# Taking the two VectorE operations on a finished attention part apart: subtraction two chunks behind, addition four

## The chip, the cores and the metric

The kernel runs on one core of one Trainium2 chip. The metric is the device time of one execution in microseconds (us), the lower the better. The kernel before was timed in three runs: median 3198.25 us, from 3195.41 to 3200.84 us.

## What is computed

One inference step of a two-layer encoder over 1024 prompt positions and 32 sample positions (1056 columns), in fp32 throughout. Layer 0 has latent attention with 16 heads, layer 1 forgetting attention with 16 heads. For this change only the core of both matters:

```
sc = q @ k.T + bias, masked
pr = softmax(sc, axis=-1)
o  = pr @ v          # one block of 64 rows per head
y  = o @ w_o         # the projection behind attention
```

After it come a gated feed-forward block of inner width 2816 and a gated per-layer embedding, in both layers.

## The kernel before, in words

**Numbers as two halves.** To keep fp32 accuracy the kernel splits each factor of a matmul into a rounded high half and the remainder (`act_hi`, `act_lo`). A product is then three matmuls (`three`, L1034 to L1036: high by high, low by high, high by low).

**Tiles, steps, heads, pairs.** In attention a head is cut into nine query tiles, 0 to 7 of 128 prompt rows and tile 8 of the 32 sample rows. They are taken in the order 7, 6, 8, 0, 5, 4, 1, 2, 3 (`ORDER`, L178), one per *step*. Two heads of nine steps make a *pair* (18 steps); the pairs run in a hardware loop (`pair`, one copy on each engine: L1245 TensorE, L1696 ScalarE, L2256 VectorE). The first pair stands ahead of the loop, and a short *drain* finishes the last head behind it.

**One step's way.** TensorE makes the scores of a tile in PSUM banks 0 to 3 (`scores`, L1155). VectorE takes the negated row maximum (`neg_max`, L2227), ScalarE the exponential with its row sum (`exps`, L1678, tile `probs`), VectorE the reciprocal of the sum (L2235), GpSimd scales the row (L931). The scores of a later tile may only enter a bank when the exponential that last read it is done (`pe.wait_ge(at_e, ...)`, L1163): tile 1 goes into bank 2, which the exponential of tile 5 frees one and a half steps earlier.

**Chunks.** The scaled probabilities must be turned before they can be multiplied with v. That is done in 11 *chunks* per head of up to four 128x128 blocks: chunks 0 to 3 belong to tiles 6 and 7, chunk 4 to tile 8, chunks 5 to 7 to tiles 4 and 5, chunk 8 to tiles 0 and 1, chunks 9 and 10 to tiles 2 and 3. TensorE turns a chunk into bank 4 or 5 (`turn`, L1208), ScalarE rounds it to its high half (`hi`, L1687, tile `probs_t_hi`), VectorE makes the low half (`lo`, L2240, tile `probs_t_lo`), and TensorE multiplies both halves with v (`pv`, L1232) into bank 6 or 7, `PV_LAG` = 2 chunks behind the turn. `RUN_STEPS` says in which step a chunk is handled; a head's chunks run on into the next head's steps, so chunks 5 to 10 of one head are handled in steps 0 to 4 of the next. Below, a chunk number with a dash (0') is of that next head.

**Leaving attention.** After chunks 4, 7 and 10 a *part* of the head's output stands complete in PSUM (32 columns in bank 6, 512 in bank 7, 512 in bank 6), as 128 rows: 64 from the high half of v, 64 from the low half. `OUT_LAG` = 2 chunks behind, ScalarE copies the upper 64 rows, rounded, to `act_hi` (`outs`, L1690 to L1694). VectorE's own `outs` (L2243) then does two operations, both reading PSUM: `out_partial` = low rows minus `act_hi` (L2252), and `act_lo` = high rows plus `out_partial` (L2254). Between them stands a wait on `at_oadd`, which the subtraction raises, as the addition reads what it wrote. The addition raises `at_olo`. TensorE waits for `at_olo` before it begins to fill a bank again (L1221): chunk 0' of the next head needs part 7 gone from bank 7, chunk 8 needs part 4 gone from bank 6, chunk 4' needs part 10 gone from it. The projection behind attention waits for the last `at_olo` (L1423).

**VectorE's order.** Within a step: `neg_max` of the step's tile, the reciprocal of the step before, then for each of the step's chunks c: `lo(c)`, `outs(c - 2)`. So the two operations on part 4 stand behind `lo(6)`, those on part 7 behind `lo(9)`, and those on part 10 behind `lo(1')` and ahead of `lo(2')`. Behind part 7's two comes `neg_max` of tile 5. Each engine works off its list in that order.

Of the kernel before, what the change touches and what calls it, by code (L numbers as in the profile page):

```python
# [15 lines left out]
F32 = mybir.dt.float32  # L16
F32R = mybir.dt.float32r
ACT = mybir.ActivationFunctionType
ALU = mybir.AluOpType
# [5 lines left out]
SEQ, DEC, PAST = 1024, 32, 256  # L25
# [7 lines left out]
H = 16  # L33
Q_RANK, KV_RANK, NOPE, ROPE, VD = 512, 256, 64, 32, 64
# [144 lines left out]
STEPS = len(ORDER)  # L179
PAIR = 2 * STEPS  # L180
TURN_SLOTS = 4
PV_LAG, OUT_LAG = 2, 2
RUNS = [(6, 7), (8,), (4, 5), (0, 1), (2, 3)]
RUN_STEPS = [5, 6, 6, 7, 8, 9, 10, 11, 12, 12, 13]
DRAIN = 5
# [14 lines left out]
HC = len(CHUNKS)  # L200
# [100 lines left out]
def build_program(nc, io):  # L301
    with ExitStack() as ctx:
# [14 lines left out]
        nh, o = at("act_hi", [P, KD, T], F32R, o)  # L317
# [161 lines left out]
        at_oadd = sem("at_o_lo_added")  # L479
# [70 lines left out]
        def last_tile(c):  # L550
            return max(chunk(c)[0], key=ORDER.index)

        def out_part(c, i, buf, half=0):

            tile = last_tile(c)
            hp = c // HC
            rows = slice(64 * (hp % 2), 64 * (hp % 2) + 64)
            pair = i + (-1 if c < 0 else 0)
            part = OUT_AFTER[tile]
            of = slice(half * VD, (half + 1) * VD)  # L560
            cols, src = ((slice(SEQ, T), ps[of, 6, 0:DEC]) if tile == 8 else
                         (slice(512, SEQ), ps[of, 7, :]) if tile > 3 else (slice(0, 512), ps[of, 6, :]))
            return buf[rows, pair, cols], src, 3 * hp + part + 1

        def score_tile(tile):
            M = P if tile < 8 else DEC
# [2 lines left out]
        def is_out(c):  # L569
            return chunk(c)[3] and last_tile(c) in OUT_AFTER  # L570
# [1455 lines left out]
        def _(dve):  # L2026
# [193 lines left out]
            def attention(layer):  # L2220
                base_n, base_c = layer * H * STEPS, layer * H * HC

                def neg_max(i, s):
                    k, tile = s % STEPS, ORDER[s % STEPS]
                    M = P if tile < 8 else DEC
                    dve.wait_ge(at_s, i * PAIR + (base_n + s + 1))
                    V.tensor_reduce(nmx[0:M, k:k + 1], score_tile(tile), AX.X, ALU.max, negate=True).then_inc(at_nm, 1)  # L2227

                def invert(i, s, first):
                    k, tile = s % STEPS, ORDER[s % STEPS]  # L2230
                    M = P if tile < 8 else DEC
                    dve.wait_ge(at_e, i * PAIR + (base_n + s + 1))
                    if not (first and s < STEPS):
                        dve.wait_ge(at_p, i * PAIR + (base_n + s - STEPS + 1))
                    V.reciprocal(rinv[0:M, k:k + 1], rsum[0:M, k:k + 1]).then_inc(at_r, 1)  # L2235

                def lo(i, c):
                    dve.wait_ge(at_hi, i * (2 * HC) + (base_c + c + 1))
                    for (dst, src), (hi, _) in zip(turned(c, ptl), turned(c, pth)):
                        last = V.tensor_tensor(dst, src, hi.bitcast(F32), ALU.subtract)  # L2240
                    last.then_inc(at_lo, 1)

                def outs(i, c):  # L2243
                    if is_out(c):
                        dst, src, n = out_part(c, i, nl)
                        dve.wait_ge(at_ohi, i * 6 + (3 * layer * H + n))
                        hp, src_cols = c // HC, src.shape[-1]
                        part = osum[64 * (hp % 2):64 * (hp % 2) + VD, 0:src_cols]
                        _, src_lo, _ = out_part(c, i, nl, 1)
                        if not (isinstance(i, int) and i == 0 and n == 1):  # L2250
                            dve.wait_ge(at_olo, i * 6 + (3 * layer * H + n - 1))
                        V.tensor_tensor(part, src_lo, out_part(c, i, nh)[0].bitcast(F32), ALU.subtract).then_inc(at_oadd, 1)  # L2252
                        dve.wait_ge(at_oadd, i * 6 + (3 * layer * H + n))
                        V.tensor_tensor(dst, src, part, ALU.add).then_inc(at_olo, 1)  # L2254

                def pair(i, first, drain=False):  # L2256
                    for s in range(DRAIN if drain else PAIR):
                        if not drain:
                            neg_max(i, s)
                        todo = [s - 1] if (s >= 1 or not first) and not (drain and s > 0) else []  # L2260
                        while todo:
                            invert(i, todo.pop(), first)
                        for c in chunks_at(s):
                            if c >= 0 or not first:
                                lo(i, c)
                            if c >= OUT_LAG or not first:
                                outs(i, c - OUT_LAG)
                    if drain:
                        for c in range(-OUT_LAG, 0):
                            outs(i, c)  # L2270

                pair(0, True)
                with dve.Fori(1, H // 2) as i:
                    pair(i, False)
                pair(H // 2, False, True)
# [530 lines left out]
```

## Time and profile before

| | us |
|---|---|
| median of three runs (lowest, highest) | 3198.25 (3195.41, 3200.84) |
| the profiled execution | 3194.3 |
| its span | 3192.5 |
| TensorE matmul busy | 3006.4 (94%) |
| VectorE busy | 2026.4 (63%) |
| GpSimd busy | 1428.1 (45%) |
| ScalarE busy | 982.6 (31%) |
| mean granted TensorE clock | 0.974 of full |

The shares are means over stages with different limits. Attention takes two stretches of the span, about 282 to 590 us (layer 0) and 1824 to 2128 us (layer 1); the feed-forward blocks take most of the rest, with TensorE busy throughout. In the rows below the time of an instruction and its length stand first; in square brackets is how long its engine sat idle before it, and what ended that.

### The profile page before, as it was taken

Reading aid. Unit: us, or ns where it says so; the run is one execution under the profiler, and the core shown is the slowest. Engines: PE = TensorE matmul, PEld = TensorE weight load, DVE = VectorE, ACT = ScalarE, POOL = GpSimd, SP = SyncE. Lnnn points to the kernel's source line nnn. Section 1 sums busy time; section 2 is a strip of 40 time slices with the busy share of each in tenths; the row PEclk is TensorE's granted clock in tenths of the full one; section 3 lists DMA queues with packets and bytes.
Section 4 is the critical chain, followed back from the end, with each engine's and each line's share of the span. In section 5 each row is a group of like instructions: output and inputs, shape, how many; then the busy total and the mean of one; then the engine's idle time right before and its main releaser. Section 6 shows DMA issues by size and latency. Waiting matters only on the chain.

```text
span 3192.5 us, 54358 instructions
## 1 busy us (share of the span) xinstructions
PE 3006.4 (94%) x18978; PEld 2905.2 (91%) x18978; DVE 2026.4 (63%) x3685; ACT 982.6 (31%) x2197; POOL 1428.1 (45%) x933
## 2 busy tenths in 40 slices
PE   8999999999999999998989999889899999999887
PEld 7889888888999999998878888889899999999887
DVE  4566888465655565567565588855655655565675
ACT  4234777342000000004442277753300000000252
POOL 4233545464333343345554455545533333343563
PEclk9999999999999999999999999999899999999998
DMA  3497444211111111111103666522011111111111
GB/s 111 178 316 242 123 122 126 98 40 47 40 53 39 46 53 39 46 46 61 40 21 127 187 138 140 130 81 73 28 53 44 42 53 39 46 52 40 48 54 55
DMA packets 163132, 264.63 MB, mean 83 GB/s; under 512 B 95057, under 2 KB 108897, under 8 KB 162641
## 3 DMA queue, kind: packets, MB, share of 16 engines
q1 hardware_dynamic: 163024, 263.21, 26.8%
q8 instruction: 66, 1.08, 0.1%
q14 instruction: 42, 0.34, 0.0%
HBM read 197.74 MB, written 65.42 MB: 82 GB/s over the span
## 4 chain that ended last, share of the span: by engine, by line
PE 78%; DVE 9%; issue 4%; ACT 4%; POOL 3%; DMA 1%; SPq 0%; DVEq 0%; ACTq 0%; POOLq 0%
PE ps L1324 30%; PE ps L1034 12%; PE ps L1035 12%; PE ps L1036 12%; PE ps L1232 4%; PE ps L1208 3%; POOL pre_sums L891 1%; DVE sublayer_out L2058 1%; PE ps L1180 1%; DVE neg_max L2227 1%; DVE out_partial L2252 1%; PE ps L1055 1%; PE ps L1181 1%; PE ps L1069 1%; ACT probs_t_hi L1687 1%
## 5 line engine op out<-in xcount | busy, mean ns | idle before, releaser
L855 POOL TENSOR_TENSOR weight_hi<-weight_raw,ones 128x1024 fp32r<-128x1024 f32 x179 | 354.9, 1982 | 1169.0 <-PE ps L1036 598.8
L2295 DVE TENSOR_TENSOR sublayer_out<-ps,sublayer_out 128x352 f32<-128x352 f32 x1008 | 527.8, 524 | 516.4 <-PE ps L1036 507.9
L1324 PE MATMUL ps<-act_hi,weight_hi 128*128 128x352 f32 x2112 | 686.1, 325 | 10.1 <-ACT ffn_act L1735 4.8
L1324 PE MATMUL ps<-act_hi,weight_lo 128*128 128x352 f32 x2112 | 683.8, 324 | 0.0
L1324 PE MATMUL ps<-act_lo,weight_hi 128*128 128x352 f32 x2112 | 683.7, 324 | 0.0
L869 POOL TENSOR_TENSOR weight_lo<-weight_raw,weight_hi 128x1024 fp32r<-128x1024 f32 x193 | 477.1, 2472 | 54.9 <-ACT weight_hi L1725 28.1
L1034 PE MATMUL ps<-act_hi,weight_hi 128*128 128x352 f32 (+2 forms) x1392 | 469.7, 337 | 29.6 <-DVE weight_lo L2102 11.4
L1035 PE MATMUL ps<-act_lo,weight_hi 128*128 128x352 f32 (+2 forms) x1392 | 457.1, 328 | 0.0
L1036 PE MATMUL ps<-act_hi,weight_lo 128*128 128x352 f32 (+2 forms) x1392 | 456.8, 328 | 0.0
L931 POOL TENSOR_TENSOR probs<-probs,row_inv 128x1024 f32<-128x1024 f32 (+8 forms) x288 | 311.0, 1092 | 322.8 <-DVE row_inv L2235 321.6
L1324 PEld LDWEIGHTS ps<-act_hi,weight_hi 128*128 128x128 f32 x2112 | 399.2, 189 | 14.4 <-issue 6.9
L1324 PEld LDWEIGHTS ps<-act_lo,weight_hi 128*128 128x128 f32 x2112 | 400.0, 189 | 0.4 <-issue 0.2
L1324 PEld LDWEIGHTS ps<-act_hi,weight_lo 128*128 128x128 f32 x2112 | 399.9, 189 | 0.5 <-issue 0.2
L1034 PEld LDWEIGHTS ps<-act_hi,weight_hi 128*128 128x128 f32 (+2 forms) x1392 | 266.4, 191 | 37.4 <-issue 22.7
L1035 PEld LDWEIGHTS ps<-act_lo,weight_hi 128*128 128x128 f32 (+2 forms) x1392 | 266.9, 192 | 4.9 <-issue 1.1
L1036 PEld LDWEIGHTS ps<-act_hi,weight_lo 128*128 128x128 f32 (+2 forms) x1392 | 266.0, 191 | 2.4
L1735 ACT ACTIVATE ffn_act<-ps 128x352 f32<-128x352 f32 x132 | 61.3, 465 | 619.3 <-DVE ps L2299 619.2
L2240 DVE TENSOR_TENSOR probs_t_lo<-ps,probs_t_hi 128x512 fp32r<-128x512 f32 (+3 forms) x384 | 210.8, 556 | 47.3 <-ACT probs_t_hi L1687 41.2
L1678 ACT ACTIVATE probs<-ps,neg_max 128x1024 f32<-128x1024 f32 (+8 forms) x288 | 204.9, 711 | 105.9 <-DVE neg_max L2227 104.6
L2227 DVE TENSOR_REDUCE neg_max<-ps 128x1 f32<-128x1024 f32 (+8 forms) x288 | 205.9, 715 | 34.5 <-PE ps L1185 32.7
L1232 PE MATMUL ps<-probs_t_hi,v_both 128*128 128x256 f32 (+3 forms) x736 | 212.6, 309 | 12.5 <-DVE probs_t_lo L2240 11.4
L1687 ACT ACTIVATE probs_t_hi<-ps 128x512 fp32r<-128x512 f32 (+3 forms) x384 | 184.5, 490 | 66.8 <-PE ps L1208 48.1
(177 smaller groups left out, 5763.1 us busy)
## 6 DMA issues: line engine op xcount, KB each, us to landing
weight_raw<-units SPq DMA_DIRECT2D x201, 512.0 KB, 3.3
k_hi<-kB_hi SPq DMA_DIRECT2D x32, 328.0 KB
qA_hi<-stage_hi SPq DMA_DIRECT2D x16, 528.0 KB, 3.4
qA_lo<-stage_lo SPq DMA_DIRECT2D x16, 528.0 KB, 4.5
q_hi<-qA_hi SPq DMA_DIRECT2D x16, 528.0 KB
q_lo<-qA_lo SPq DMA_DIRECT2D x16, 528.0 KB
kA_hi<-stage_hi SPq DMA_DIRECT2D x8, 656.0 KB, 3.0
kA_lo<-stage_lo SPq DMA_DIRECT2D x8, 656.0 KB, 4.7
```

The source lines that it names most:

```text
L855: pool.tensor_tensor(wh[:, slot, :], wraw[:, slot, :], ones[:, 0:1].to_broadcast((P, UW)), ALU.mult).then_inc(w_hi[slot], 1)
L869: pool.tensor_tensor(wl[:, slot, :], wraw[:, slot, :], wh[:, slot, :].bitcast(F32), ALU.subtract).then_inc(w_rdy[slot], 1)
L931: pool.tensor_tensor(p, p, rinv[0:M, k:k + 1].to_broadcast((M, KEYS[tile])), ALU.mult).then_inc(at_p, 1)
L1034: nc.tensor.matmul(out, ah, bh, start=first, stop=False)
L1035: nc.tensor.matmul(out, ah, bl, start=False, stop=False)
L1036: return nc.tensor.matmul(out, al, bh, start=False, stop=last)
L1232: mm = nc.tensor.matmul(out, halves, p.rearrange("p t q -> p (t q)") if n > 1 else p[:, 0, :], start=kt == 0 and h == 0, stop=ends and j + ...
L1324: mm = nc.tensor.matmul(ps[:, 3 * slot + b, 0:TB], a, x, start=(k == 0 and pas == 0), stop=(k == KD - 1 and pas == 2))
L1687: last = nc.scalar.activation(dst, src, ACT.Copy)
L2227: V.tensor_reduce(nmx[0:M, k:k + 1], score_tile(tile), AX.X, ALU.max, negate=True).then_inc(at_nm, 1)
L2240: last = V.tensor_tensor(dst, src, hi.bitcast(F32), ALU.subtract)
L2295: V.tensor_tensor(y[:, m, c], src, y[:, m, c], ALU.add).then_inc(f_acc, 1)
```

## The change

The subtraction stays where it was, two chunks behind. The addition gets a lag of its own, four chunks, and is issued behind `lo(c)` and ahead of the subtraction of the same turn. Semaphores and their counts stay; ScalarE's and TensorE's programs are not touched. The addition on part 4 now stands behind `lo(8)`, that on part 7 behind `lo(0')`, that on part 10 behind `lo(3')`. The drain issues the addition on part 7 behind its last `lo`.

```diff
-PV_LAG, OUT_LAG = 2, 2
+PV_LAG, OUT_LAG, LOW_LAG = 2, 2, 4
...
+        def out_sum(c):
+
+            rows = slice(64 * (c // HC % 2), 64 * (c // HC % 2) + VD)
+            return osum[rows, 0:DEC if last_tile(c) == 8 else 512]
...
-                def outs(i, c):
+                def out_partial(i, c):
+
+                    if is_out(c):
+                        _, src_lo, n = out_part(c, i, nl, 1)
+                        dve.wait_ge(at_ohi, i * 6 + (3 * layer * H + n))
+                        if not (isinstance(i, int) and i == 0 and n == 1):
+                            dve.wait_ge(at_olo, i * 6 + (3 * layer * H + n - 1))
+                        V.tensor_tensor(out_sum(c), src_lo, out_part(c, i, nh)[0].bitcast(F32),
+                                        ALU.subtract).then_inc(at_oadd, 1)
+
+                def out_low(i, c):
+
                     if is_out(c):
                         dst, src, n = out_part(c, i, nl)
-                        dve.wait_ge(at_ohi, i * 6 + (3 * layer * H + n))
-                        hp, src_cols = c // HC, src.shape[-1]
-                        part = osum[64 * (hp % 2):64 * (hp % 2) + VD, 0:src_cols]
-                        _, src_lo, _ = out_part(c, i, nl, 1)
-                        if not (isinstance(i, int) and i == 0 and n == 1):
-                            dve.wait_ge(at_olo, i * 6 + (3 * layer * H + n - 1))
-                        V.tensor_tensor(part, src_lo, out_part(c, i, nh)[0].bitcast(F32), ALU.subtract).then_inc(at_oadd, 1)
                         dve.wait_ge(at_oadd, i * 6 + (3 * layer * H + n))
-                        V.tensor_tensor(dst, src, part, ALU.add).then_inc(at_olo, 1)
+                        V.tensor_tensor(dst, src, out_sum(c), ALU.add).then_inc(at_olo, 1)
...
                         for c in chunks_at(s):
                             if c >= 0 or not first:
                                 lo(i, c)
+                            if c >= LOW_LAG or not first:
+                                out_low(i, c - LOW_LAG)
                             if c >= OUT_LAG or not first:
-                                outs(i, c - OUT_LAG)
+                                out_partial(i, c - OUT_LAG)
                     if drain:
-                        for c in range(-OUT_LAG, 0):
-                            outs(i, c)
+                        for c in range(-LOW_LAG, 0):
+                            out_low(i, c)
+                            if c + LOW_LAG - OUT_LAG < 0:
+                                out_partial(i, c + LOW_LAG - OUT_LAG)
```

## Rows read from the trace of the kernel before

**Rows 1.** The page: busy time of each engine, its share of the span, instructions

```profile
PE 3006.4 (94%) x18978; PEld 2905.2 (91%) x18978; DVE 2026.4 (63%) x3685; ACT 982.6 (31%) x2197; POOL 1428.1 (45%) x933
```

**Rows 2.** Waits in attention of layer 0: total us, times, longest us

```profile
PE ps L1034 <- ACT probs L1678: 11.8, 16, 1.2
```

**Rows 3.** Waits in attention of layer 1, same columns

```profile
PE ps L1180 <- ACT probs L1678: 22.5, 16, 2.1
```

**Rows 4.** Timeline of VectorE, layer 0, a pair's first head: start, length

```profile
359.94 0.69 DVE L2240 TENSOR_TENSOR probs_t_lo<-ps,probs_t_hi 128x512 fp32r<-128x512 f32 x1 [0.94 <-ACT probs_t_hi L1687]
360.67 0.69 DVE L2252 TENSOR_TENSOR out_partial<-ps,act_hi 64x512 f32<-64x512 f32 x1
361.49 0.68 DVE L2254 TENSOR_TENSOR act_lo<-ps,out_partial 64x512 f32 x1
362.20 0.96 DVE L2227 TENSOR_REDUCE neg_max<-ps 128x1 f32<-128x768 f32 x1
...
364.71 0.69 DVE L2240 TENSOR_TENSOR probs_t_lo<-ps,probs_t_hi 128x512 fp32r<-128x512 f32 x1
365.31 0.41 DVE L2227 TENSOR_REDUCE neg_max<-ps 128x1 f32<-128x256 f32 x1
```

**Rows 5.** The same in the pair's second head

```profile
379.53 0.69 DVE L2252 TENSOR_TENSOR out_partial<-ps,act_hi 64x512 f32<-64x512 f32 x1
...
380.96 0.94 DVE L2227 TENSOR_REDUCE neg_max<-ps 128x1 f32<-128x768 f32 x1
```

**Rows 6.** Timeline of TensorE in the first head, and one stall of the second

```profile
364.24 0.39 PE L1034 MATMUL ps<-k_hi,q_hi 128*128 128x256 f32 x1 [1.03 <-ACT probs L1678]
...
366.00 0.36 PE L1232 MATMUL ps<-probs_t_hi,v_both 128*128 128x256 f32 x1
...
369.14 0.35 PE L1232 MATMUL ps<-probs_t_hi,v_both 128*128 128x256 f32 x1 [0.27 <-DVE probs_t_lo L2240]
...
382.97 0.39 PE L1034 MATMUL ps<-k_hi,q_hi 128*128 128x256 f32 x1 [0.43 <-ACT probs L1678]
```

**Rows 7.** Timeline of VectorE, layer 1, a pair's second head

```profile
1926.41 0.69 DVE L2240 TENSOR_TENSOR probs_t_lo<-ps,probs_t_hi 128x512 fp32r<-128x512 f32 x1 [0.22 <-ACT probs_t_hi L1687]
...
1929.82 0.67 DVE L2240 TENSOR_TENSOR probs_t_lo<-ps,probs_t_hi 128x512 fp32r<-128x512 f32 x1
...
1932.86 1.22 DVE L2227 TENSOR_REDUCE neg_max<-ps 128x1 f32<-128x1024 f32 x1 [0.49 <-PE ps L1185]
```

**Rows 8.** Timeline of TensorE in that head

```profile
1925.95 0.38 PE L1180 MATMUL ps<-k_hi,q_hi 128*128 128x256 f32 x1 [1.10 <-ACT probs L1678]
...
1927.60 0.36 PE L1232 MATMUL ps<-probs_t_hi,v_both 128*128 128x256 f32 x1
...
1930.64 0.35 PE L1232 MATMUL ps<-probs_t_hi,v_both 128*128 128x256 f32 x1 [0.59 <-DVE probs_t_lo L2240]
```

**Rows 9.** Timeline of TensorE, layer 1: stalls of first and of second heads, in turn

```profile
1907.21 0.58 PE L1180 MATMUL ps<-k_hi,q_hi 128*128 128x256 f32 x1 [1.82 <-ACT probs L1678]
...
2055.78 0.38 PE L1180 MATMUL ps<-k_hi,q_hi 128*128 128x256 f32 x1 [1.81 <-ACT probs L1678]
...
2074.25 0.38 PE L1180 MATMUL ps<-k_hi,q_hi 128*128 128x256 f32 x1 [1.10 <-ACT probs L1678]
...
2092.82 0.39 PE L1180 MATMUL ps<-k_hi,q_hi 128*128 128x256 f32 x1 [1.81 <-ACT probs L1678]
...
2110.67 0.38 PE L1180 MATMUL ps<-k_hi,q_hi 128*128 128x256 f32 x1 [1.10 <-ACT probs L1678]
```

**Rows 10.** Windows behind these stalls: busy by engine, then granted clock, DMA share, GB/s

```profile
1907.21:1911.21 4.00, 4.00 (x21) 4.00 (x22) 2.78 (x7) 3.15 (x8) 2.68 (x2) 0.57 0.05 11
...
1925.95:1929.95 4.00, 4.00 (x32) 3.80 (x32) 3.45 (x9) 3.58 (x9) 2.68 (x2) 1.00 0.35 81
...
2092.82:2096.82 4.00, 4.00 (x32) 3.81 (x32) 3.53 (x8) 3.73 (x9) 2.68 (x2) 1.00 0.34 77
```

**Rows 11.** Timeline of VectorE in layer 0's drain

```profile
587.12 0.56 DVE L2240 TENSOR_TENSOR probs_t_lo<-ps,probs_t_hi 128x384 fp32r<-128x384 f32 x1
```

## The prediction

> **What bounds the kernel now.** I read the page first: TensorE is busy for 94% of the span, VectorE for 63% [rows 1]. That is a mean. In the feed-forward stages TensorE has no gap to give, and the change issues nothing there. So I went on to the waits of the two attention stretches, the only place where L2252 and L2254 run. There TensorE waits in every head for the exponential that frees its score bank: 11.8 us in 16 times in layer 0 [rows 2], 22.5 us in 16 times in layer 1 [rows 3]. ScalarE in turn was released by `neg_max`. What holds `neg_max` back? The timeline of VectorE shows it: `lo(9)` at 359.94, the subtraction on part 7 at 360.67, its addition at 361.49, and only then `neg_max` of tile 5 at 362.20 [rows 4], whose scores had long been there. TensorE takes up the scores of tile 1 at 364.24, after 1.03 us of idling, and stalls again, 0.27 us, at 369.14, where `pv` waits for `lo(2')` [rows 6], which stands behind part 10's two operations in the same way. I call these site A (behind part 7) and site B (behind part 10). The pattern repeats through both layers: at A a pair's first head (7 of them per layer, as the first pair has nothing to finish there) stalls 1.03 us in layer 0 and 1.8 in layer 1, the second head (8 per layer) 0.43 and 1.10 [rows 6, 8, 9]. At B second heads of layer 1 stall 0.59 [rows 8].
>
> The six first heads of layer 1 up to 2055.78 pay something more: behind the 1.82 us stall TensorE is granted 0.57 of its clock, that is mostly the 1.2 GHz level, for about 4 us. Behind the last such stall it is granted all of it, as it is in each second head, after 1.10 us [rows 10].
>
> **The change part by part.** Nothing is removed: 96 subtractions and 96 additions stay, 64 of each 64x512 and 0.68 to 0.69 us long, 32 small ones of 64x32. No DMA and no other engine's list is touched. The additions change place.
>
> *Site A, what is freed.* From subtraction to `neg_max` it is 1.53 us in a first head (360.67 to 362.20 [rows 4]), 1.43 in a second (379.53 to 380.96 [rows 5]). With the addition gone `neg_max` follows the subtraction itself. The trace has no such pair. From below, `neg_max` starts 0.60 us behind a 512-wide operation of its own partitions (364.71 to 365.31), from above 0.82 behind it (the addition's distance, 360.67 to 361.49), and `lo` to subtraction, where the rows read from PSUM change as they would here, is 0.73 [all rows 4]. I take 0.72, as it is that nearest case: `neg_max`, the exponential and the scores of tile 1 come 0.81 us earlier in first heads and 0.71 in second heads. Bounds 0.6 to 0.9.
>
> The Trainium skill bears on that choice: VectorE: DVE Perf Modes, section Two Vector instructions with no wait between them, gives as a model that an operation starts before the end of the last one unless its start quadrant differs from that of the last read or write. By it 0.72 is right here, since the subtraction reads PSUM from row 64 and `neg_max` from row 0. If `neg_max` overlapped all the same, 0.60 would hold and A would give 0.1 us more a head.
>
> *Site A, what comes back.* The addition on part 7 now stands behind `lo(0')`, and `pv(0')` may not fill bank 7 before it is done. Layer 0, first head: `lo(0')` at 364.71 comes 0.81 earlier, 363.90. The addition starts 0.72 later, 364.62, ends 365.30, and a VectorE result reaches TensorE 0.14 later (the lag behind `lo(2')`, which ends 368.99, to 369.14): 365.44. TensorE would be at `pv(0')` at 366.00 less 0.81, 365.19 [rows 6]. **A new stall of 0.25 us.** Layer 1, second head: `lo(0')` 1926.41 [rows 7] less 0.71 is 1925.70; addition at 1926.31 (0.61 behind, its partitions are `lo`'s), end 1926.99, ready 1927.13, against 1927.60 [rows 8] less 0.71, 1926.89: stall 0.24. In first heads of layer 1, where the rows follow rows 4 in kind, the same sum gives 0.38. Layer 0's second head had only 0.43 to give at A [rows 6]; TensorE comes at its `pv(0')` so late that no stall arises.
>
> *Site B.* `neg_max` of tile 1 stood at `lo(0')` plus 0.60; it now stands behind the addition, so it keeps nearly its old time, and so do `lo(1')` and subtraction 10, which come only some 0.4 us earlier. But `lo(2')` loses the addition ahead of it, 0.82 us more. Layer 1, second head: new `lo(2')` at about 1928.76, against 1929.82 [rows 7], done for TensorE at 1929.60. TensorE arrives at 1930.64 less 0.59, less 0.71, plus 0.24: 1929.58 [rows 8]. The stall of 0.59 is gone, and the head has gained 1930.64 less 1929.60, **1.04 us**. Layer 0, first head: 0.81 plus 0.27 less 0.25 is **0.83**. Layer 0, second head: 0.43, and 0.07 for a gap at B too short to be listed: **0.5**.
>
> *The additions' new places.* Part 10's addition goes between `lo(3')` and `neg_max` of tile 3. VectorE idles 0.49 us before `neg_max` of tile 7 [rows 7]; TensorE wants to be 1.04 earlier there, VectorE comes only about 0.66 earlier. The exponential behind it then frees its bank a tenth of a microsecond late for tile 8's scores: I take 0.1 off each head of layer 1. Part 4's addition, 0.18 us long, goes behind `lo(8)` into the idling before `lo(9)`, which is 0.94 us in a first head [rows 4] and about half of that in a second; without that cover it would cost 16 times 0.2 us a layer. `pv(8)`, which waits for it, comes over half a microsecond later.
>
> *The clock.* The stall of 1.8 us in first heads of layer 1 falls to 1.0, with 0.38 following it. Since 1.10 with 0.59 behind it never lowered the clock in second heads, I count it as kept. From stall to stall the first heads at the lower level take 18.74 us (1907.21 to 1925.95) down to 18.47 (2055.78 to 2074.25), the one at full clock 17.85 (2092.82 to 2110.67) [rows 8, 9]: 0.6 to 0.9, taken as 0.73, six times. Bounds: nothing, and 5.4 us.
>
> *Drain.* `lo(10)`, at 587.12 [rows 11], stood behind the addition, which takes 0.68 us [rows 4]; it comes 0.7 us earlier, in both layers. The addition fits under `pv(10)`.
>
> **The sum.** Layer 0: 8 x 0.5 + 7 x 0.83 = 9.8. Layer 1: 8 x (1.04 - 0.1) + 7 x (1.05 - 0.1) = 14.2 (first heads at full clock come out at 1.05 in the same way). Clock 6 x 0.73 = 4.4. Drains 1.4. Together 29.8 us. The profiled execution took 3194.3 us with a span of 3192.5, and would come to 3164.5; the median of the runs lies 3.95 above it, so I forecast 3198.25 - 29.8 = 3168.5.
>
> **The rivals.**
>
> *The new wait at `pv(0')` doesn't bite, and VectorE keeps up* (0.15). Then 7 x 0.25 + 7 x 0.38 + 8 x 0.24 + 15 x 0.1 = 7.8 us come back as gain: 3160.7. For it: the stalls rest on differences of a quarter microsecond. Against: the additions stand where I put them.
>
> *Half the gain is taken by the loop around VectorE* (0.17). In layer 1 it has 0.49, 0.22 and about 0.5 to 0.9 us of idling per head [rows 4, 7], and 1.04 us is more than it can follow unless the chain `turn`, `hi`, `lo(9)` comes earlier too. If only the gap between subtraction and addition and half of A arrive, 0.45 us in each of 31 heads and none of the clock, that is 14 us: 3184.
>
> *The order of the same work doesn't matter* (0.04). If VectorE's total set the pace, the time would fall only by the gap that a wait adds (0.82 against 0.73, 64 times): 5.8 us, 3192.5. Against: TensorE's stalls end on one `neg_max`, and VectorE idles elsewhere in each head. The Trainium skill's VectorE: DVE Perf Modes, section The DRAIN you can't avoid, says that a semaphore between VectorE operations costs nothing extra and that their count is what to lower; by that alone the result would be 3198.25, as the count stays.
>
> *Slower: `pv(0')` becomes the stall that lowers the clock* (0.04). Its place is bank 7: if the addition came more than 0.8 us after TensorE wants the bank, A would be lost, and two stalls close together would drop the clock in all 31 heads and not in six. 25 x 0.73 = 18 us more, and nothing gained: 3216. It decides from a stall at `pv(0')` of about 0.8 us; I find 0.24 to 0.38.
>
> **How the numbers follow.** My own case has 0.60; it runs from 3162 to 3175 with the bounds of A, the clock and the runs' scatter. 3160.7 and 3184 join it for the range: 3157 to 3186, which leaves out 0.08 above and a little more below and between. A measurement here can tell about 0.2%, 6.4 us, from no change: faster 0.92, the same 0.04, slower 0.04.
>
> **What would show it.** In the profile after, VectorE at part 7 should read subtraction, `neg_max` 0.72 us behind, and TensorE's wait for `probs` should fall to about 0.2 us in layer 0's first heads and none in its second, to 1.0 and 0.4 in layer 1. A wait of `pv` (L1232) for L2254's successor should appear, 0.24 to 0.38 us. The waits for `probs_t_lo` at B should go. The windows behind layer 1's first-head stalls should read a clock of 1.00. I am wrong if the stretches of attention, 308 and 304 us long, shorten by less than 5 and 12 us, if the clock still falls, or if something outside attention moves.

## The result, and the profile after

The changed kernel takes 3167.41 us (median of six runs, 3164.58 to 3174.06), the kernel before in the same session 3195.56 (six runs, 3190.70 to 3200.84): a ratio of 0.9913, 95% interval 0.9898 to 0.9927, or 28 us less. The forecast was 3168.5. The profiled execution took 3167.9 us with a span of 3166.1, against 3194.3 and 3192.5 before: 26.4 us less, against 29.8 in the sum.

The page of the changed kernel, busy time by engine:

```profile
PE 3004.7 (95%) x18978; PEld 2901.6 (92%) x18978; DVE 2039.4 (64%) x3685; ACT 982.9 (31%) x2197; POOL 1426.3 (45%) x933
```

Every engine issues as many instructions as before [rows 1], and no busy time falls by more than 4 us. What went is mostly idling of TensorE: in attention 26.3 of the 31.1 us below. Windows over the two attention stretches, from the first scores to the first matmul of the projection: first the kernel before, then the changed one. The columns are the stretch and its length, the busy time of TensorE, its weight loads, VectorE, ScalarE and GpSimd, then granted clock, DMA share and GB/s.

```profile
280.12:590.53 310.41, 290.56 (x2112) 264.00 (x2113) 256.60 (x578) 217.83 (x530) 161.69 (x148) 1.00 0.44 116
1823.81:2128.14 304.33, 271.45 (x1921) 245.32 (x1921) 255.26 (x576) 213.57 (x528) 161.71 (x148) 0.94 0.56 127
```

```profile
280.86:577.33 296.47, 288.25 (x2112) 264.03 (x2112) 258.92 (x578) 218.33 (x530) 162.24 (x148) 1.00 0.45 122
1816.97:2104.14 287.17, 268.96 (x1920) 237.71 (x1921) 255.74 (x576) 212.70 (x528) 162.19 (x148) 0.98 0.58 134
```

(Layer 0's begins at 280.12, so it was 310.4 us long before, not 308.) Layer 0 gives 13.9 us, layer 1 17.2, together 31.1. The profiled execution as a whole gave 26.4, so 4.7 us went the other way outside attention. The stretch between the two attentions, where the change issues nothing, is 1233.3 us in the execution profiled before and 1239.6 after. But it is 1238.4 and 1239.5 us in two other profiles of kernels that time like the one before (`before_again` and `only4`, below), and 1235.0 to 1240.4 in ten more, all of the change or of a variant of it: scatter between executions, and no price of the change that these profiles can tell.

TensorE's waits: what waited, what for, us in total, times, longest. First the wait of `pv` for `lo` in the kernel before, layer 0 (280 to 591 us) and layer 1 (1823 to 2129 us):

```profile
PE ps L1232 <- DVE probs_t_lo L2240: 3.9, 9, 1.3
PE ps L1232 <- DVE probs_t_lo L2240: 7.5, 12, 1.3
```

The changed kernel, layer 0 (280 to 580 us):

```profile
PE ps L1039 <- ACT probs L1683: 2.8, 8, 1.2
PE ps L1237 <- DVE probs_t_lo L2245: 1.3, 2, 0.7
```

And layer 1 (1810 to 2100 us, ahead of the drain's last two waits):

```profile
PE ps L1185 <- ACT probs L1683: 11.6, 16, 1.3
PE ps L1237 <- DVE act_lo L2263: 1.6, 7, 0.2
```

The wait for the exponential is 2.8 us where it was 11.8, and 11.6 where it was 22.5 [rows 2, 3]. Of the waits for `lo` at `pv` (now L1237) only two in each layer's drain are left. A wait of `pv` for `act_lo` is new. L2255 is now the subtraction, L2263 the addition. VectorE's timeline in layer 0, a pair's first head:

```profile
358.08 0.69 DVE L2245 TENSOR_TENSOR probs_t_lo<-ps,probs_t_hi 128x512 fp32r<-128x512 f32 x1 [0.81 <-ACT probs_t_hi L1692]
358.81 0.69 DVE L2255 TENSOR_TENSOR out_partial<-ps,act_hi 64x512 f32<-64x512 f32 x1
359.54 0.96 DVE L2232 TENSOR_REDUCE neg_max<-ps 128x1 f32<-128x768 f32 x1
...
362.04 0.69 DVE L2245 TENSOR_TENSOR probs_t_lo<-ps,probs_t_hi 128x512 fp32r<-128x512 f32 x1
362.76 0.68 DVE L2263 TENSOR_TENSOR act_lo<-ps,out_partial 64x512 f32 x1
363.48 0.42 DVE L2232 TENSOR_REDUCE neg_max<-ps 128x1 f32<-128x256 f32 x1
```

`neg_max` of tile 5 starts 0.73 us behind the subtraction, where it was 1.53 [rows 4]; the addition has its place behind `lo(0')`. TensorE's timeline: two first heads of layer 0 with the second head between them, then layer 1.

```profile
361.57 0.39 PE L1039 MATMUL ps<-k_hi,q_hi 128*128 128x256 f32 x1 [0.23 <-ACT probs L1683]
...
379.62 0.30 PE L1039 MATMUL ps<-k_hi,q_hi 128*128 128x256 f32 x1
...
397.75 0.39 PE L1039 MATMUL ps<-k_hi,q_hi 128*128 128x256 f32 x1 [0.23 <-ACT probs L1683]
...
1896.26 0.39 PE L1185 MATMUL ps<-k_hi,q_hi 128*128 128x256 f32 x1 [1.02 <-ACT probs L1683]
...
1898.38 0.36 PE L1237 MATMUL ps<-probs_t_hi,v_both 128*128 128x256 f32 x1 [0.23 <-DVE act_lo L2263]
...
1913.61 0.39 PE L1185 MATMUL ps<-k_hi,q_hi 128*128 128x256 f32 x1 [0.42 <-ACT probs L1683]
```

The stall for tile 1's scores is 0.23 and none in layer 0, where it was 1.03 and 0.43 [rows 6], and 1.02 and 0.42 in layer 1, where it was 1.8 and 1.10 [rows 8, 9]. A pair is 36.18 us long in layer 0 (361.57 to 397.75), before 38.02. In layer 1 it is 34.73 on average, before 37.15. Behind layer 1's first-head stalls the clock now stands (columns as in rows 10):

```profile
1896.26:1900.26 4.00, 3.77 (x29) 3.42 (x30) 3.75 (x9) 3.60 (x9) 2.72 (x2) 1.00 0.31 71
```

That holds for all seven, where it fell in six before [rows 10].

### The profile page after: what moved, and what is told of

Its sections match the earlier page's. It is cut to its first block, busy times and chain, and to the rows that moved or that the text cites. A ratio compares the mean times of both kernels' runs of the same rounds, so it can differ in the third digit from the quotient of the medians.

```text
span 3166.1 us, 54358 instructions
## 1 busy us (share of the span) xinstructions
PE 3004.7 (95%) x18978; PEld 2901.6 (92%) x18978; DVE 2039.4 (64%) x3685; ACT 982.9 (31%) x2197; POOL 1426.3 (45%) x933
## 4 chain that ended last, share of the span: by engine, by line
PE 65%; issue 13%; POOL 11%; DVE 6%; ACT 2%; DMA 1%; POOLq 0%; SPq 0%; DVEq 0%; ACTq 0%
PE ps L1329 31%; PE ps L1039 11%; PE ps L1040 11%; PE ps L1041 11%; POOL probs L936 8%; DVE sublayer_out L2063 1%; PE ps L1060 1%; POOL pre_sums L896 1%; PE ps L1074 1%; DVE act_lo L2078 1%; POOL weight_hi L860 1%; DVE post_sums L2039 1%; DVE pre_sums L2039 1%; DVE stage_lo L2162 1%; DMA kA_lo<-stage_lo 1%
## 5 line engine op out<-in xcount | busy, mean ns | idle before, releaser
L1237 PE MATMUL ps<-probs_t_hi,v_both 128*128 128x256 f32 (+3 forms) x736 | 209.0, 305 | 4.9 <-DVE probs_t_lo L2245 2.6
```

Source lines behind the costliest of these rows:

```text
L1237: mm = nc.tensor.matmul(out, halves, p.rearrange("p t q -> p (t q)") if n > 1 else p[:, 0, :], start=kt == 0 and h == 0, stop=ends and j + ...
```

## The experiments

Most of them give each part's addition its own lag, with the lags as a table by the part's last tile (8 is part 4, 4 is part 7, 3 is part 10). The changed kernel is `{8: 4, 4: 4, 3: 4}`, the one before has 2 throughout; the drain issues what is left through the same helper. Shown with the lags of `only7`:

```diff
-PV_LAG, OUT_LAG, LOW_LAG = 2, 2, 4
+PV_LAG, OUT_LAG = 2, 2
+LOW_LAGS = {8: 2, 4: 4, 3: 2}
...
+                def out_after(i, c, first, end=PAIR * HC):
+                    for lag in (5, 4, 3, 2):
+                        if lag == OUT_LAG and (c >= OUT_LAG or not first) and c - OUT_LAG < end:
+                            out_partial(i, c - OUT_LAG)
+                        if (c >= lag or not first) and c - lag < end and LOW_LAGS.get(last_tile(c - lag)) == lag:
+                            out_low(i, c - lag)
```

In one table first, attention (the two stretches, in one profiled execution each) and the timed ratio to the kernel before:

| kernel | layer 0, us | layer 1, us | ratio [95% interval] |
|---|---|---|---|
| before | 310.4 | 304.3 | 1 |
| `before_again` | 310.9 | 301.8 | one run, 3191.95 us |
| changed | 296.5 | 287.2 | 0.9913 [0.9898, 0.9927] |
| `after_again` | 296.4 | 288.7 | 0.9907 [0.9887, 0.9927] |
| `only7` | 305.0 | 295.5 | 0.9953 [0.9936, 0.9969] |
| `only10` | 305.2 | 297.5 | 0.9955 [0.9940, 0.9970] |
| `only4` | 310.5 | 302.7 | one run, 3197.81 us |
| `lag3` | 299.4 | 295.3 | 0.9923 [0.9903, 0.9944] |
| `lag5at7` | 316.0 | 298.9 | 1.0003 [0.9994, 1.0013] |
| `pad_at_a` | 307.0 | 297.4 | 0.9961 [0.9946, 0.9976] |
| `pad_in_idle` | 300.7 | 290.9 | 0.9932 [0.9912, 0.9951] |
| `rowmax_first` | 296.9 | 282.4 | 0.9892 [0.9873, 0.9912] |
| `late10` | 295.8 | 285.0 | 0.9903 [0.9883, 0.9923] |
| `both` | 296.3 | 280.2 | 0.9882 [0.9866, 0.9899] |

The kernels before had medians of 3196.21 us (14 runs, beside `only7`, `only10`, `lag3`, `lag5at7`), 3197.36 (8 runs, beside the pads, `rowmax_first` and `only4`) and 3194.29 (7 runs, beside the rest).

**Part 7's addition alone is moved (`only7`: `{8: 2, 4: 4, 3: 2}`).**

> Only the addition on part 7 is moved to four chunks behind; those on parts 4 and 10 stay directly behind their subtractions. Theory (a late row maximum at A, a late low half at B, and the clock): nearly all of A and the clock in layer 1's first heads, little of B. Per head against before: layer 0 about 0.4 us, layer 1 about 0.3, plus six times 0.73 for the clock and 0.7 for each drain: about 16.5 us, so a ratio to the kernel before near 0.995. TensorE's stall at A as in the changed kernel; the wait for probs_t_lo at B stays, above 0.3 us; the clock behind layer 1's first-head stalls reads 1.00. Rival (the gap of the wait alone): 32 large gaps of 0.09 us less, 3 us. Rival (VectorE's total sets the pace): no change.

Measured: 3181.39 us, ratio 0.9953 [0.9936, 0.9969], by the ratio 15.0 us of gain. TensorE's timeline in layer 1:

```profile
1906.02 0.39 PE L1186 MATMUL ps<-k_hi,q_hi 128*128 128x256 f32 x1 [1.02 <-ACT probs L1684]
...
1911.54 0.36 PE L1238 MATMUL ps<-probs_t_hi,v_both 128*128 128x256 f32 x1 [0.81 <-DVE probs_t_lo L2246]
```

Site A reads as in the changed kernel (1.02, and 0.23 at `pv(0')`, 1908.14), and none of the seven first-head stalls is followed by a fall of the clock. Site B keeps its stall, and a longer one: 0.81 here, where the one first head of layer 1 that kept its clock before had 0.72, and 0.54 in layer 0's first heads for 0.27. What A freed arrives at B and is partly lost there.

**Part 10's addition alone (`only10`: `{8: 2, 4: 2, 3: 4}`).**

> Only the addition on part 10 is moved; part 7's addition stays ahead of the row maximum of tile 5. Theory: A stays whole (stalls of 1.03 and 0.43 us in layer 0, 1.8 and 1.1 in layer 1), B's stalls go, the clock still falls to the lower level behind six stalls. About 8 us less than before, ratio near 0.9975. If A and B were not separate, this would give half of the whole change, 14 us. Rival (gap alone): 3 us. Rival (VectorE's total): no change.

Measured: 3182.73 us, 0.9955 [0.9940, 0.9970], 14.4 us by the ratio, where 8 were expected. Layer 0's attention is 5.2 us shorter than before and layer 1's 6.9. Over seven pairs 5.2 us are 0.74 a pair, while the only idling that the trace of before lists at B in layer 0 is 0.27 in first heads [rows 6]. Windows of TensorE behind the first two first-head stalls of layer 1 (its busy time, clock, DMA share, GB/s):

```profile
1865.10:1869.10 4.00, 4.00 (x23) 0.63 0.31 73
1901.51:1905.51 4.00, 4.00 (x32) 1.00 0.34 79
```

The clock falls behind every other stall, four of the seven, where six were expected, although site A is untouched. A pair with the fall is 36.41 us (1865.10 to 1901.51), one without 35.52 (1901.51 to 1937.03).

**Part 4's alone (`only4`: `{8: 4, 4: 2, 3: 2}`).**

> Only part 4's addition, the small one of 64x32, is moved. Theory: its 0.3 us on VectorE ahead of the row maximum of tile 8 are covered in both layers or nearly so: the stalls at A and B as before, 0 to 2 us less than before. If VectorE's chain in steps 1 to 3 mattered (in layer 1's first heads turn(9) begins at the end of lo(7)), up to 0.3 us in each of 15 heads, 4 us.

One run, 3197.81 us, beside 3197.36 for the median before. The attention stretches are as before. Moving the 64x32 additions gives and takes nothing that one run can tell. By the ratios `only7` and `only10` account for the changed kernel: 15.0 and 14.4 us come to 29.4 and the change gave 28. The traces are sharper, and there the two sites are not simply added. In layer 0, where no clock falls, a pair takes 37.41 us in `only7` (362.46 to 399.87), 37.27 in `only10` (362.03 to 399.30), 38.02 before and 36.18 in the changed kernel: 0.61 and 0.75 alone, 1.84 together. At the full clock in layer 1 it is 0.47 and 0.86 alone (35.91 and 35.52 for 36.38) and 1.65 together. The 0.3 to 0.5 us on top fit what `only7` shows: A frees them and the longer stall at B takes them back, so site A pays in full only with B cleared.

**The kernel before once more (`before_again`, no edit).**

> The kernel before, for a second profile. The stretch between the two attention stages took 1233.3 us in its first profile and 1239.6 in that of the changed kernel. Theory: this is scatter of the stage ahead of layer 1's attention, which the change doesn't touch, so here it may come out anywhere from 1233 to 1240; the attention stretches themselves read 310.4 and 304.3 us again within 1 us. Rival (the change makes that stage slower by 6 us): 1233 again.

Windows of TensorE behind two first-head stalls of layer 1:

```profile
1871.69:1875.69 4.00, 4.00 (x32) 1.00 0.34 78
1908.07:1912.07 4.00, 4.00 (x21) 0.57 0.11 25
```

A stall of the same kind (2.06 us ahead of the first window, 1.8 ahead of the second) is followed by a fall of the clock at one head and not at another; four of seven fell here, six in the first profile. Layer 1's attention is 2.5 us shorter than in the first profile, which is more than the 1 us expected; two falls fewer are 1.4 of it. From stall to stall the head at full clock takes 17.81 us, the other (1908.07 to 1926.58) 18.51, a price of 0.70.

**The changed kernel once more (`after_again`, no edit).**

> The changed kernel itself once more, beside the two above on one chip, as what they are measured against: ratio to before 0.991.

Measured: 3167.35 us, 0.9907 [0.9887, 0.9927]; no fall of the clock behind any stall of this kind, as in the first profile.

**All additions at lag 3 (`lag3`).**

> All three additions three chunks behind in place of four. Part 7's is then behind lo(10) and ahead of the row maximum of tile 4. Theory: the row maximum of tile 5 is as early as with four; the wait of pv(0') for bank 7 goes, but the row maximum of tile 4 and its exponential come 0.6 us later than with four, which ScalarE hands on to hi(1'), lo(1') and lo(2'); so the time is that of the changed kernel within 5 us, about 28 us less than before (ratio 0.991), with other stalls. If the wait for bank 7 were what holds the changed kernel back, lag 3 would be 5 us or more faster than it.

Measured: 3174.20 us, 0.9923 [0.9903, 0.9944], which in time alone can't be told from the changed kernel. Its attention is 11 us longer in the profiles, and the profiled execution is the slowest of its four. Part 7's addition now stands between `lo(10)` and `neg_max` of tile 4. Rows of VectorE, ScalarE and TensorE there, layer 1:

```profile
1932.37 0.68 DVE L2264 TENSOR_TENSOR act_lo<-ps,out_partial 64x512 f32 x1
1933.08 0.82 DVE L2233 TENSOR_REDUCE neg_max<-ps 128x1 f32<-128x640 f32 x1
1933.94 0.79 ACT L1684 ACTIVATE probs<-ps,neg_max 128x640 f32<-128x640 f32 x1 [0.74 <-DVE neg_max L2233]
1934.74 1.12 PE L1214 MATMUL ps<-ident,probs 128*128 128x128 f32 x4 [0.55 <-DVE probs_t_lo L2246]
```

It makes the next `neg_max` late; ScalarE idles 0.74 us for it, and TensorE stalls 0.55 us at a turn, 2 us behind the stall of 1.02 at site A. And here the clock falls, behind four of the seven such pairs of stalls. TensorE's windows behind the 0.55 us stall in two first heads in turn:

```profile
1899.26:1903.26 4.00, 3.77 (x28) 1.00 0.74 168
1934.74:1938.74 4.00, 4.00 (x20) 0.58 0.74 168
```

From first-head stall to first-head stall a pair with the fall takes 36.13 us (1932.76 to 1968.89), one without 35.49 (1897.27 to 1932.76). Four falls at 0.64 are thus 2.6 of the 11 us. The rest is the order itself: a pair of layer 0, without any fall, takes 36.58 us (361.37 to 397.95) for 36.18, one of layer 1 at the full clock 35.49 for 34.73. So it isn't the mere separation of the two operations that pays, but which `neg_max` or `lo` the addition stands ahead of.

**Part 7's addition one chunk later still (`lag5at7`: `{8: 4, 4: 5, 3: 4}`).**

> As the changed kernel, but part 7's addition five chunks behind, after lo(1'). Theory: the row maximum at A is as early as with four, but pv(0') now waits for bank 7 some 1.2 to 1.6 us in every head and gives A back: layer 0 loses 0.5 to 0.65 us a head against before, layer 1 about 0.1; the drains give 1.4. About 4 to 9 us slower than before, ratio 1.001 to 1.003, and if the longer idling lowers the clock in more heads, up to 15 us more. Rival (the addition is hidden wherever it stands): as the changed kernel, ratio 0.991.

Measured: 3198.14 us, 1.0003 [0.9994, 1.0013]: the whole gain is gone, though TensorE lists no wait for `lo` at site B, as in the changed kernel. The 4 to 9 us more than before that were expected didn't come. TensorE's timeline, a first and a second head of layer 0, then a head of layer 1:

```profile
404.43 0.35 PE L1238 MATMUL ps<-probs_t_hi,v_both 128*128 128x256 f32 x1 [1.45 <-DVE act_lo L2264]
...
423.42 0.39 PE L1238 MATMUL ps<-probs_t_hi,v_both 128*128 128x256 f32 x1 [1.14 <-DVE act_lo L2264]
...
1916.77 0.36 PE L1238 MATMUL ps<-probs_t_hi,v_both 128*128 128x256 f32 x1 [1.50 <-DVE act_lo L2264]
```

The wait at `pv(0')` for bank 7 exists in every head and is paid in full. Layer 0's attention comes out 5.6 us longer than before, layer 1's 5.4 shorter. The window behind that 1.50 us stall:

```profile
1916.77:1920.77 4.00, 4.00 (x28) 1.00 0.62 137
```

The clock stays at its full level, in all seven pairs of layer 1. Layer 1 was expected to lose 0.1 us a head. With the full clock its pair takes 36.35 us (17.98 and 18.37) against 36.38 before (`before_again`), so the 5.4 us are, nearly all, the six falls that are gone and the drain's 0.7.

**A VectorE operation more at site A (`pad_at_a`).** The result of the added operation isn't read by anything.

```diff
+                def pad(c):
+                    rows = slice(64 * ((c // HC + 1) % 2), 64 * ((c // HC + 1) % 2) + VD)
+                    V.tensor_tensor(osum[rows, :], res[rows, 0, 0:512], res[rows, 1, 0:512], ALU.add)
...
                                 out_partial(i, c - OUT_LAG)
+                            if c % HC == 9 and (c >= 0 or not first) and not drain:
+                                pad(c)
```

> The changed kernel with one more VectorE operation per head, a 64x512 addition on SBUF whose result nothing reads, directly behind part 7's subtraction and so ahead of the row maximum of tile 5. 31 are issued, some 0.6 us each. Theory (it is the place that counts): the stall at A grows by that much in every head and B moves with it, in layer 1 VectorE's chain from lo(9) to lo(2') is 0.6 longer: 15 x 0.6 in layer 1 = 9 us, in layer 0 about 0.6 in first heads and 0.3 in second ones, 6.5 us: 15 us slower than the changed kernel, about 3182, ratio to before 0.996. Rival (the amount counts, the place doesn't): the same as pad_in_idle.

Measured: 3186.67 us, 0.9961 [0.9946, 0.9976]. VectorE's timeline, layer 1 (L2268 is the added one):

```profile
1905.12 0.69 DVE L2255 TENSOR_TENSOR out_partial<-ps,act_hi 64x512 f32<-64x512 f32 x1
1905.84 0.68 DVE L2268 TENSOR_TENSOR out_partial<-residual 64x512 f32<-64x512 f32 x1
1906.54 0.96 DVE L2232 TENSOR_REDUCE neg_max<-ps 128x1 f32<-128x768 f32 x1
```

TensorE's stall behind it:

```profile
1908.58 0.39 PE L1185 MATMUL ps<-k_hi,q_hi 128*128 128x256 f32 x1 [1.60 <-ACT probs L1683]
```

`neg_max` is 1.42 us behind the subtraction, the stall 1.60 in place of 1.02, and attention 20.8 us longer than in the changed kernel, where 15 were expected. One of the seven 1.60 us stalls lowered the clock.

**The same operation in idle time (`pad_in_idle`).** `pad(c)` is issued ahead of `lo(c)`, where VectorE waits in the changed kernel (0.81 us at 358.08, above).

```diff
+                            if c % HC == 9 and (c >= 0 or not first) and not drain:
+                                pad(c)
                             if c >= 0 or not first:
                                 lo(i, c)
```

> The same extra operation, but ahead of lo(9), where VectorE idles 0.5 to 0.8 us before that operation in the changed kernel. Theory: hidden in first heads, 0.1 to 0.2 late in second ones; about 3 us slower than the changed kernel, 3170, ratio 0.992. Rival (VectorE's total sets the pace): 31 x 0.6 = 19 us in both kernels with a pad.

Measured: 3173.89 us, 0.9932 [0.9912, 0.9951]; attention is 7.9 us longer than in the changed kernel, not 20.8. VectorE's timeline, layer 1, a first and a second head:

```profile
1889.85 0.73 DVE L2268 TENSOR_TENSOR out_partial<-residual 64x512 f32<-64x512 f32 x1
1890.63 0.69 DVE L2245 TENSOR_TENSOR probs_t_lo<-ps,probs_t_hi 128x512 fp32r<-128x512 f32 x1
...
1907.59 0.96 DVE L2268 TENSOR_TENSOR out_partial<-residual 64x512 f32<-64x512 f32 x1
```

TensorE's stalls behind them:

```profile
1894.12 0.39 PE L1185 MATMUL ps<-k_hi,q_hi 128*128 128x256 f32 x1 [0.91 <-ACT probs L1683]
...
1912.04 0.38 PE L1185 MATMUL ps<-k_hi,q_hi 128*128 128x256 f32 x1 [0.98 <-ACT probs L1683]
```

`lo(9)` now follows the added operation without a wait, so the idle time was used up. The same operation, the same 30 times (15 in each layer), costs 13 us less here than two operations further down the queue. It still costs a quarter of a microsecond a head, and the lines say where: in second heads. VectorE idles only 0.46 us there ahead of `lo(9)` (0.81 in first heads), the added operation takes 0.92 to 0.97 us there (0.73 in first heads, 0.69 everywhere in `pad_at_a`), and TensorE's stall is 0.98 in place of 0.42, while in first heads it is 0.91 in place of 1.02. Why the operation is longer there is open.

**The subtraction behind `neg_max` of tile 5 (`rowmax_first`).** Additions as in the change; part 7's subtraction goes one chunk later.

```diff
-                        if lag == OUT_LAG and (c >= OUT_LAG or not first) and c - OUT_LAG < end:
-                            out_partial(i, c - OUT_LAG)
+                        if lag in (2, 3) and (c >= lag or not first) and c - lag < end:
+                            if lag == (3 if last_tile(c - lag) == 4 else 2):
+                                out_partial(i, c - lag)
```

> The changed kernel with part 7's subtraction three chunks behind in place of two: the row maximum of tile 5 stands directly behind lo(9) and ahead of the subtraction, so it and its exponential come another 0.72 us earlier. The stall at A then falls to 0.3 us in layer 1's first heads and to none elsewhere. If A's stall still set the time, that would give 0.23 in each first head of layer 0, 0.7 and 0.4 in layer 1: 10 us. Theory: in layer 1 VectorE's work from lo(9) to lo(2') is now the longest way and its length doesn't change, so pv(0') waits longer for bank 7 what A waits less: a gain of 2 to 4 us at most, within what can be told from the changed kernel.

Measured: 3163.57 us, 0.9892 [0.9873, 0.9912]. VectorE's timeline, layer 1:

```profile
1923.58 0.69 DVE L2246 TENSOR_TENSOR probs_t_lo<-ps,probs_t_hi 128x512 fp32r<-128x512 f32 x1 [0.81 <-ACT probs_t_hi L1693]
1924.19 0.95 DVE L2233 TENSOR_REDUCE neg_max<-ps 128x1 f32<-128x768 f32 x1
...
1925.69 0.69 DVE L2256 TENSOR_TENSOR out_partial<-ps,act_hi 64x512 f32<-64x512 f32 x1
```

TensorE's, behind it:

```profile
1928.08 0.66 PE L1214 MATMUL ps<-ident,probs 128*128 128x128 f32 x4 [0.44 <-DVE probs_t_lo L2246]
...
1928.98 0.36 PE L1238 MATMUL ps<-probs_t_hi,v_both 128*128 128x256 f32 x1 [0.25 <-DVE act_lo L2264]
```

The stall for tile 1's scores is gone altogether. In its place come 0.44 us at a turn and 0.25 at `pv(0')`. Layer 1's pair falls from 34.73 to 34.10 us; layer 0's, which had 0.23 left at A, doesn't gain (36.26 against 36.18). The ratio's interval touches the changed kernel's, so this gain rests on the traces.

**Part 10's addition one chunk later (`late10`: `{8: 4, 4: 4, 3: 5}`).** In layer 1's first heads the changed kernel showed an idling of TensorE that I hadn't placed there. Its chain, in rows of VectorE, ScalarE and TensorE:

```profile
2040.74 0.69 DVE L2263 TENSOR_TENSOR act_lo<-ps,out_partial 64x512 f32 x1
2041.46 0.69 DVE L2232 TENSOR_REDUCE neg_max<-ps 128x1 f32<-128x512 f32 x1
2042.19 0.69 ACT L1683 ACTIVATE probs<-ps,neg_max 128x512 f32<-128x512 f32 x1 [1.01 <-DVE neg_max L2232]
...
2043.02 0.50 PE L1185 MATMUL ps<-k_hi,q_hi 128*128 128x512 f32 x1
```

Part 10's addition stands ahead of `neg_max` of tile 3, ScalarE idles 1.01 us for it, and TensorE takes up the scores of the next head's tile 6 some 0.3 us late.

> The changed kernel with part 10's addition five chunks behind, behind lo(4') and so behind the row maximum of tile 3 in place of ahead of it. Theory: in the changed kernel TensorE loses 0.3 us in each first head of layer 1, where the scores of the next tile 6 wait for the exponential of tile 3, late because the addition stands ahead of that row maximum. Here that exponential comes 0.6 us earlier and the 0.3 goes: 2 us in layer 1, nothing in layer 0; 3165, a ratio to before of 0.9905 to 0.991. If the row maximum of tile 7 were what is late, nothing would change, as it stays where it was.

Measured: 3160.14 us, 0.9903 [0.9883, 0.9923]. The same rows in that kernel:

```profile
2032.95 0.68 DVE L2233 TENSOR_REDUCE neg_max<-ps 128x1 f32<-128x512 f32 x1
2033.67 0.69 ACT L1684 ACTIVATE probs<-ps,neg_max 128x512 f32<-128x512 f32 x1 [0.17 <-DVE neg_max L2233]
```

The addition now starts behind `neg_max`, at 2033.94. ScalarE's idling is 0.17, the scores of tile 6' come 0.29 us earlier behind the stall at A, and a pair of layer 1 takes 34.48 us instead of 34.73; layer 0's stays at 36.18. The ratio's interval covers the changed kernel's, so in time alone the two can't be told apart.

**The two last edits together (`both`).**

> The row maximum of tile 5 ahead of part 7's subtraction, as in rowmax_first, and part 10's addition five chunks behind, as in late10. If the two are separate, 2 us less than rowmax_first: about 3161, ratio 0.9885. If VectorE's chain from lo(9) on is the bound in layer 1 whatever the order, the same as rowmax_first.

Measured: 3158.59 us, 0.9882 [0.9866, 0.9899], against 3167.35 for `after_again` on the same chip. Layer 1's pair is 33.86 us. The intervals of `both` and `after_again` overlap a little, so the 9 us between the medians rest on the traces too: attention takes 576.5 us in `both` against 583.6 and 585.1 in the two profiles of the changed kernel. It beats the kernel before by 1.2%.

## Why the prediction was right, point by point

**The mechanism held.** The wait for `probs` was taken as VectorE's order and not its load. `only7`, `lag3` and the two pads show that: what counts is what stands ahead of one `neg_max`. The rival by which the order doesn't matter falls with `pad_at_a` against `pad_in_idle`, 13 us apart for the same operation. The count of VectorE's operations, by which alone the time would have stayed at 3198.25, is the same before and after, 3685. The rival by which VectorE's loop takes half the gain stood at 3184, and the time is 3167.41. (It and the slow rival counted 31 heads; the sum's own 7 and 8 a layer make 30, which moves neither by a microsecond.)

Below, a shift is measured from start to start between the same two instructions in both kernels.

**Site A.** Taken: 0.72 from subtraction to `neg_max`. Measured: 0.73 (358.81 to 359.54). The scores of tile 1 come 0.80 us earlier in first heads of both layers (forecast 0.81); the stall goes from 1.03 to 0.23 and from 1.8 to 1.02. In second heads of layer 1 it is 0.68 (0.71). Layer 0's second head gave 0.59 where I allowed the listed 0.43.

**The new stall at `pv(0')`.** Forecast 0.25 in layer 0's first heads, 0.38 in layer 1's, 0.24 in its second heads. From the scores of tile 1 to `pv(0')` TensorE now takes 2.11 us in the first (361.57 to 363.68; before 1.76) and 2.12 in the second (1896.26 to 1898.38; before, at the full clock, 1.64 from 2092.82): 0.35 and 0.48, though the profile lists nothing and 0.23. In the third some 0.2 us are lost. So the new stall was sized 0.1 too small in first heads. The rival that it doesn't bite is out; `lag5at7` shows what it costs when it bites fully.

**Site B was sized too small in layer 0.** The term was 0.27 in first heads and 0.07 in second; measured, 0.44 and 0.32. `only10` shows it by itself: 0.74 us a pair, where these two add up to 0.76. The listed idle time had been taken as the whole wait. So the sum for layer 0 (9.8 and 0.7 of drain) fell 3.4 us short of the 13.9 measured. In layer 1's second heads it was 0.58 with the change and 0.66 in `only10`, against 0.59.

**Layer 1's new cost had the wrong place and size.** I put 0.1 us a head at `neg_max` of tile 7 and tile 8's scores. It was 0.3 us in first heads, at `neg_max` of tile 3 and tile 6's scores, as `late10` shows by removing it; 0.25 of it reaches the pair. Between pairs that both have the full clock, layer 1 gained 1.65 us (36.38 in `before_again`, 1871.69 to 1908.07, less 34.73), against 0.94 + 0.95 = 1.89 in the sum.

**The clock.** Kept, as forecast: no fall in the three profiles of `only7` and of the changed kernel (two). But the reason given, that 1.10 with 0.59 behind it never lowered the clock, doesn't carry so far: there the two stalls lie 4.7 us apart (1925.95 to 1930.64). In `lag3` a stall of 1.02 with 0.55 behind it, 2 us apart, lowered it four times in seven. In the changed kernel 0.23 is listed in that place. That it kept the clock was thus partly luck: nothing in the rows of before showed that the new pair of stalls was on the safe side. The price of 0.73 was fair (0.70 in `before_again`). But six falls are no property of the kernel: `before_again` and `only4` had four. By that the term is 2.9 to 4.4 us. The slower rival, two stalls close together that lower the clock, is half borne out: its large stall at `pv(0')` came in `lag5at7` without a fall (behind 1.50 us the clock stayed, and the loss there is the stall alone), its fall in `lag3` at another place.

**Drain.** `lo(10)` starts 1.45 us behind the `lo` before it, before 2.17: 0.72 earlier, as forecast.

**The sum.** Attention gave 31.1 us in the first profiles, 29.3 with each kernel's two profiles averaged, and the forecast was 29.8. Layer 0 was too small by 3.4 and layer 1 (14.2, 4.4 and 0.7) too large by 2.1: the total is nearer than its parts deserve. With the two profiles averaged layer 1 gave 15.1, and its sum was too large by 4.2. The prediction also counted a move outside attention as a sign of being wrong. The 4.7 us there are such a move, and only the profiles taken later put it down to scatter.

## What to carry to other kernels

In a queue that is worked off in order, an operation's price is what stands behind it: sort what can wait behind what another engine needs next, and give each of two dependent operations the latest place that its own consumer allows. That place has an edge on either side here, a chunk earlier (`lag3`) losing a little in the traces and a chunk later (`lag5at7`) all of it, so find from the trace who waits for each and check the neighbouring slots one by one. When a wait is gone, read who is late next before moving anything else; twice that gave the next step here (`late10`, `rowmax_first`).

## What the runs showed of the hardware that I had not expected

- Whether a stall of 1.8 to 2.1 us lowers TensorE's clock varies within one execution and between executions of one kernel: six, four, four and four of seven (the kernel before twice, `only4`, `only10`). A stall of 1.60 us did in one of seven (`pad_at_a`). Stalls of 1.02 with 0.55 listed 2 us later did in four of seven (`lag3`), stalls of 1.02 with 0.23 there in none (the changed kernel twice), nor did the pairs of 1.02 and 1.50 us in `lag5at7`. So the length of the stall alone doesn't decide it, and what does is open here.
- Ahead of a matmul the listed idle time is less than the wait: the second heads' scores of layer 0 came 0.59 us earlier where 0.43 of idling was listed, and 0.44 where 0.27 was. In the new stall at `pv(0')` nothing was listed for 0.35 and 0.23 for 0.48. Between 0.16 and 0.25 us are missing each time, which fits the page's note that the ends of matmuls are modelled. Shifts between two kernels are better measured from start to start.
- `neg_max` starts 0.61 us behind `lo` (1923.58 to 1924.19 in `rowmax_first`) and 0.73 behind the subtraction (358.81 to 359.54), though both operations ahead of it last 0.69 us. That fits the rule of the Trainium skill that the prediction weighed, in VectorE: DVE Perf Modes, section Two Vector instructions with no wait between them: the subtraction reads PSUM from row 64, `lo` and `neg_max` from row 0. The addition agrees, and there only the rows change: it reads PSUM from row 0 in every head, and its other operand and its result lie in rows from 64 on in first heads, from 0 on in second, and `neg_max` of tile 5 followed it before by 0.71 (361.49 to 362.20) and by 0.61 (380.35 to 380.96).
- Between subtraction and addition the kernel before has 0.82 us from start to start in the hardware loop and 0.73 outside it (585.67 to 586.40 in the drain), for the same two operations and the same wait on `at_oadd`. Outside it the wait thus costs nothing that shows, as 0.73 is also what `neg_max` needs behind the subtraction without one. In the loop the count waited for is computed from the loop's register; that this costs the 0.09 us is the likely reason and not shown by an edit.
